# A dense SwiGLU layer whose gate and up products are formed, for 12 of 22 blocks, with seven block products in place of eight

## What is computed

```python
def swiglu(h, w_gate, w_up, w_down):          # h 512 x 1024, gate and up 1024 x 2816, down 2816 x 1024
    return (jax.nn.silu(h @ w_gate) * (h @ w_up)) @ w_down
x = x + swiglu(rmsnorm(x, norm_ffn[0]), ffn_w_gate[0], ffn_w_up[0], ffn_w_down[0])
```

## Time and profile before

| what | value |
|---|---|
| median of 3 runs | 1556.56 us (1556.38 to 1557.34) |
| the profiled execution: its time | 1556.81 us |
| its span (first to last instruction) | 1555.1 us |
| PE busy | 1538.5 us, 99% of the span |
| DVE, ACT, POOL busy | 65%, 54%, 15% |
| granted TensorE clock | 0.997 of full |

### The profile page before, as it was taken

The page is one execution under the profiler, slowest core; times in us unless marked ns, Lnnn a source line. Parts: engine busy times, 40 slices in busy tenths (PEclk is TensorE's granted clock), DMA queues, the critical chain, the costliest instruction groups (busy, mean ns, idle before and its releaser), DMA issues.

```text
span 1555.1 us, 23275 instructions
## 1 busy us (share of the span) xinstructions
PE 1538.5 (99%) x7960; PEld 1309.2 (84%) x7961; DVE 1009.2 (65%) x1689; ACT 834.3 (54%) x1330; POOL 236.7 (15%) x290
## 2 busy tenths in 40 slices
PE   9999999999999999999999999999999999999997
PEld 6888888888888888888888888879898888889895
DVE  7657765755444443336557765776676988887587
ACT  6436665433223322324447664475576888886564
POOL 0204564000000000002015662010000011110000
PEclk9999999999999999999999999999999999999998
DMA  7832212244444233326322212518778999997773
GB/s 228 196 99 69 74 55 82 95 136 136 156 138 138 95 91 98 99 91 155 102 92 69 72 55 90 195 57 320 257 256 254 358 385 372 388 384 266 240 255 134
DMA packets 89787, 265.71 MB, mean 171 GB/s; under 512 B 12497, under 2 KB 22737, under 8 KB 89680
## 3 DMA queue, kind: packets, MB, share of 16 engines
q1 hardware_dynamic: 82864, 248.59, 47.1%
q0 software_dynamic: 6816, 15.74, 3.7%
HBM read 242.84 MB, written 19.83 MB: 169 GB/s over the span
## 4 chain that ended last, share of the span: by engine, by line
PE 96%; DVE 2%; DMA 1%; issue 1%; ACT 0%; SPq 0%; DVEq 0%; ACTq 0%; POOLq 0%
PE ps L1698 19%; PE ps L1703 19%; PE ps L1699 19%; PE ps L2052 8%; PE ps L2027 5%; PE ps L2029 5%; PE ps L2028 5%; PE ps L2054 3%; PE ps L1865 2%; PE ps L1898 1%; PE ps L2026 1%; PE ps L2025 1%; PE ps L1878 1%; PE ps L1897 1%; PE ps L1877 1%; PE ps L2013 1%
## 5 line engine op out<-in xcount | busy, mean ns | idle before, releaser
L808 ACT ACTIVATE w_hi<-raw 128x1024 fp32r<-128x1024 f32 (+1 forms) x168 | 176.0, 1047 | 337.1 <-PE ps L1703 333.8
L1698 PE MATMUL ps<-h_hi,w_hi 128*128 128x512 f32 x880 | 350.6, 398 | 0.6 <-DVE k_lo L1245 0.4
L1699 PE MATMUL ps<-h_lo,w_hi 128*128 128x512 f32 x880 | 343.6, 390 | 0.0
L1703 PE MATMUL ps<-h_hi,w_lo 128*128 128x512 f32 x880 | 343.4, 390 | 0.0
L1157 DVE TENSOR_TENSOR w_lo<-raw,w_hi 128x1024 fp32r<-128x1024 f32 x136 | 164.3, 1208 | 124.1 <-ACT w_hi L808 123.9
L1162 DVE TENSOR_TENSOR m_lo<-m_raw,m_hi 128x1024 fp32r<-128x1024 f32 x144 | 167.9, 1192 | 61.1 <-ACT m_hi L851 60.3
L1703 PEld LDWEIGHTS ps<-h_hi,w_lo 128*128 128x128 f32 x880 | 165.2, 188 | 35.4
L1698 PEld LDWEIGHTS ps<-h_hi,w_hi 128*128 128x128 f32 x880 | 165.6, 188 | 27.0 <-DVE k_lo L1245 0.8
L1699 PEld LDWEIGHTS ps<-h_lo,w_hi 128*128 128x128 f32 x880 | 166.0, 189 | 25.9 <-issue 0.7
L851 ACT ACTIVATE m_hi<-m_raw 128x1024 fp32r<-128x1024 f32 x144 | 145.4, 1031 | 53.0 <-PE ps L2026 25.9
L2052 PE MATMUL ps<-xt,m_hi 128*128 128x320 f32 x592 | 154.3, 347 | 0.3 <-issue 0.3
(11 more groups left out here) (308 smaller groups left out, 3161.7 us busy)
## 6 DMA issues: line engine op xcount, KB each, us to landing
m_raw<-moe_g SPq DMA_DIRECT2D x88, 512.0 KB, 5.1
raw<-w_in SPq DMA_DIRECT2D x68, 512.0 KB, 3.4
m_raw<-moe_down SPq DMA_DIRECT2D x56, 512.0 KB, 5.2
raw<-w_gu SPq DMA_DIRECT2D x44, 512.0 KB, 3.5
h_rows<-moe_g SPq DMA_DIRECT2D x32, 512.0 KB, 5.2
h_rows<-moe_g SPq DMA_DIRECT2D x32, 384.0 KB, 4.6
h_rows<-moe_down SPq DMA_DIRECT2D x24, 512.0 KB, 5.7
m_raw<-moe_g SPq DMA_DIRECT2D x24, 384.0 KB, 5.6
```

The lines of the kernel that those rows point to most:

```text
L808: A.activation(split_of(n, 0, cols)[0], raw[:, n % RAW, 0:cols], ACT.Copy).then_inc(hi_ready, 1)
L1698: E.matmul(ps[:, bank, :], wh, hi, start=first, stop=False)
L1699: E.matmul(ps[:, bank, :], wh, lo, start=False, stop=False)
L1703: return E.matmul(ps[:, bank, :], wl, hi, start=False, stop=final)
```

## The change

Twelve of the 22 pairs (f = 3, 4, 6, 7, 9, 10, 12, 13, 15, 16, 18, 19: two in turn, then one as before) are computed as a product of two-by-two blocks. The weights are split into gate and up, and each into its lower and upper half of the width; the tokens' h into lower and upper width, and into the first and second 256 tokens. With sums of weights (three tiles of 128x512: u_lo + u_hi, that minus g_lo, g_lo - u_lo, and later g_hi minus the second) and sums of tokens (four tiles of h, made once) seven products of half the width and half the tokens give the four results by additions. A block product is 4 width blocks by 3 matmuls of 128x256.

- PE: a pair of this kind ("seven") is 7 products of 12 matmuls of 128x256; a pair of the old kind stays 48 matmuls of 128x512.
- POOL makes the three sums of weights and the later fourth, and the low part of the sixth product's weights (number 5 of 0 to 6): per pair 5 instructions of 128x512.
- ACT makes seven high parts of 128x512 in place of two of 128x1024, and copies the first product's result out of PSUM (128x256).
- DVE makes the other six low parts of 128x512, and four additions (one of 128x256, three of 128x512) that read PSUM. The gate is scaled by rms_inv in place (from SBUF), the up result is not scaled; the factor is multiplied into the result of the down product instead (8 further 128x512 in PSUM, one per three down units). The work on silu and act of the two pairs stands behind the second one.
- The w_hi and w_lo buffers are handed out by halves: a block product's weights are split when the product three before it begins. The two raw buffers of a seven come free together, after its last low parts.
- The whole h (eight 128x512, ACT) and its four sums (two of 128x1024 on DVE, two on POOL) are made during pairs 0 to 2, and split into high and low (eight of 128x512 on ACT and on DVE).

The core of the diff:

```diff
+        SEVENS = [f for f in range(PLAIN, KF - 2) if (f - PLAIN) % 3 < 2]
+        JOBS = [job for f in range(KF) for job in
+                ([("seven", f, j) for j in range(7)] if f in SEVENS else [("unit", f, j) for j in range(2)])]
...
+        def seven_weights(f, j):
+
+            gate, up = FFN_START + 2 * f, FFN_START + 2 * f + 1
+            low, high = slice(0, T), slice(T, UNIT)
+            return ((gate, low), (None, 1), (None, 2), (None, 0), (gate, high), (up, high), (None, 2))[j]
...
             def load(n, src):
-                if n >= RAW:
-                    sp.wait_ge(lo_ready, n - RAW + 1)
+                m = n - RAW
+                if FFN_START + 2 <= m < FFN_END:
+                    f, j = (m - FFN_START) // 2, m % 2
+                    if f in SEVENS:
+                        sp.wait_ge(seven_lo, low_by(f))
+                        sp.wait_ge(seven_lo_pool, SEVENS.index(f) + 1)
+                    else:
+                        sp.wait_ge(seven_lo, LOW_COUNT[JOB[("unit", f, j)]])
+                elif n >= RAW:
+                    sp.wait_ge(lo_ready, m + 1)
                 sp.dma_start(raw[:, n % RAW, 0:src.shape[1]], src).then_inc(raw_full[n % RAW], 16)
...
+            def weight_sums(q, part):
+
+                f = SEVENS[q]
+                n = FFN_START + 2 * f
+                gate, up = raw[:, n % RAW, :], raw[:, (n + 1) % RAW, :]
+                split = lambda p, j: LOW_COUNT[JOB[("seven", SEVENS[p], j)]]
+                if part == 0:
+                    pool.wait_ge(raw_full[n % RAW], 16 * (n // RAW + 1))
+                    pool.wait_ge(raw_full[(n + 1) % RAW], 16 * ((n + 1) // RAW + 1))
+                    if q:
+                        pool.wait_ge(seven_lo, split(q - 1, 3))
+                    pool.tensor_tensor(sums[0][:], up[:, 0:T], up[:, T:UNIT], ALU.add).then_inc(sums_ready, 1)
+                    pool.wait_ge(sums_ready, 4 * q + 1)
+                    pool.tensor_tensor(sums[1][:], sums[0][:], gate[:, 0:T], ALU.subtract).then_inc(sums_ready, 1)
+                if part == 1:
+                    if q:
+                        pool.wait_ge(seven_lo, split(q - 1, 6))
+                    pool.tensor_tensor(sums[2][:], gate[:, 0:T], up[:, 0:T], ALU.subtract).then_inc(sums_ready, 1)
+                if part == 2:
+                    pool.wait_ge(sums_ready, 4 * q + 2)
+                    pool.wait_ge(seven_lo, split(q, 2))
+                    pool.tensor_tensor(sums[2][:], gate[:, T:UNIT], sums[1][:], ALU.subtract).then_inc(sums_ready, 1)
+
+            def low_on_pool(q):
+
+                x = JOB[("seven", SEVENS[q], 5)]
+                pool.wait_ge(seven_hi, x - 1)
+                hi, lo = job_split(x)
+                pool.tensor_tensor(lo, job_full(x), hi.bitcast(F32), ALU.subtract).then_inc(seven_lo_pool, 1)
...
+                if layer == 0:
+                    pool.wait_ge(h32_ready, KD)
+                    pool.wait_ge(t_full_ready, 2)
+                    pool.tensor_tensor(t_full(2), h_block(0, second_half), h_block(0, first_half), ALU.subtract).then_inc(t_full_ready, 1)
+                    pool.tensor_tensor(t_full(3), h_block(1, first_half), t_full(0), ALU.subtract).then_inc(t_full_ready, 1)
+                    for part in range(3):
+                        weight_sums(0, part)
+                    for q in range(1, len(SEVENS)):
+                        if q % 2:
+                            weight_sums(q, 0)
+                            low_on_pool(q - 1)
+                        else:
+                            low_on_pool(q - 1)
+                            weight_sums(q, 0)
+                        weight_sums(q, 1)
+                        weight_sums(q, 2)
+                    low_on_pool(len(SEVENS) - 1)
...
+                    def whole_h(k):
+                        A.activation(h_full(k), xs[:, k, :], ACT.Copy, scale=gains[:, gain_of(1), k:k + 1]).then_inc(h32_ready, 1)
+
+                    for k in range(KD - 2):
+                        whole_h(k)
+                    for x, (kind, f, j) in enumerate(JOBS):
+                        if x < 2:
+                            A.wait_ge(unit_done, FFN_START + x + 1)
+                        else:
+                            A.wait_ge(seven_done, x - 1)
+                        if kind == "seven" and j == 0:
+                            A.activation(quarters[:, 4 * f, :], seven_bank(f, 0), ACT.Copy).then_inc(p1_kept, 1)
+                        for y in FREED_BY[x]:
+                            job_high(y)
+                        if x >= len(JOBS) - 2:
+                            first_down(FFN_END + x - len(JOBS) + 2)
+                        if kind == "seven" and j == 6 and f + 1 not in SEVENS:
+                            silu(f - 1)
+                            silu(f)
+                            act_hi(f - 1)
+                            act_hi(f)
+                        if kind == "unit" and j == 0:
+                            silu(f)
+                        if x == 0:
+                            whole_h(KD - 2)
+                            whole_h(KD - 1)
+                        if kind == "unit" and j == 1 and f + 1 not in SEVENS:
+                            act_hi(f)
+                        if kind == "seven" and j == 0 and f - 1 not in SEVENS:
+                            act_hi(f - 1)
+                        if x in (3, 4):
+                            token_parts_hi((2 * x - 6, 2 * x - 5))
...
+                        if kind == "seven" and j == 1:
+                            V.wait_ge(p1_kept, q + 1)
+                            if q % 2:
+                                V.wait_ge(seven_sums, 4 * q)
+                            V.tensor_tensor(quarters[:, 4 * f + 2, :], quarters[:, 4 * f, :], banks[:, 2, :], ALU.add).then_inc(seven_sums, 1)
+                        if kind == "seven" and j == 3:
+                            V.wait_ge(seven_sums, 4 * q + 1)
+                            V.tensor_tensor(quarters[:, 4 * f + 1:u3_at(f) + 1:u3_at(f) - 4 * f - 1, :], twice(quarters[:, 4 * f + 2, :]),
+                                            banks[:, 4:7:2, :], ALU.add).then_inc(seven_sums, 1)
+                        if kind == "seven" and j == 5:
+                            V.wait_ge(seven_sums, 4 * q + 2)
+                            u3 = quarters[:, u3_at(f), :]
+                            if f + 1 < KF - 2:
+                                V.tensor_tensor(quarters[:, 4 * f + 2:4 * f + 4, :], twice(u3), banks[:, 3:5, :], ALU.add).then_inc(seven_sums, 1)
...
+                        if kind == "seven" and j == 6:
+                            V.tensor_tensor(quarters[:, 4 * f:4 * f + 2, :], quarters[:, 4 * f:4 * f + 2, :], banks[:, 1:8:6, :], ALU.add).then_inc(seven_sums, 1)
+                        for y in FREED_BY[x]:
+                            if not on_pool(y):
+                                job_low(y)
+                        if x >= len(JOBS) - 2:
+                            split_lo(FFN_END + x - len(JOBS) + 2)
+                        if kind == "seven" and j == 6 and f + 1 not in SEVENS:
+                            V.wait_ge(seven_sums, 4 * (q + 1))
+                            gate_scaled_in_place(f - 1)
+                            gate_scaled_in_place(f)
+                            gated_up(f - 1, act_of(f - 1))
+                            gated_up(f, act_of(f))
+                            act_lo(f - 1)
+                            act_lo(f)
+                        if kind == "unit" and j == 1:
+                            gated_up(f, ps[:, pair_banks(f)[1], :])
+                            if f + 1 not in SEVENS:
+                                act_lo(f)
+                        if kind == "seven" and j == 1 and f - 1 not in SEVENS:
+                            act_lo(f - 1)
+                        if x == 1:
+                            V.wait_ge(h32_ready, KD)
+                            V.tensor_tensor(t_full(1), h_block(1, second_half), h_block(0, second_half), ALU.subtract).then_inc(t_full_ready, 1)
+                            V.wait_ge(t_full_ready, 1)
+                            V.tensor_tensor(t_full(0), t_full(1), h_block(0, first_half), ALU.add).then_inc(t_full_ready, 1)
+                        if x in (3, 4):
+                            token_parts_lo((2 * x - 6, 2 * x - 5))
...
+                            scaled(ps[:, m % 2, :], m % 2).then_inc(ffn_scaled, 1)
+                            V.wait_ge(ffn_scaled, KF + m + 1)
                             V.tensor_tensor(xs[:, m, :], xs[:, m, :], ps[:, m % 2, :], ALU.add).then_inc(x_updated, 1)
...
+                    def block_product(x, f, j):
+                        q, out = SEVENS.index(f), seven_bank(f, j)
+                        if j == 0 and q % 2 == 0:
+                            E.wait_ge(ffn_scaled, f)
+                        if j == 1 and q == 0:
+                            E.wait_ge(act_ready, 1)
+                        if j == 3 and q % 2 == 0:
```

(24 more changed lines are left out.)

199 lines of the change are left out of this document (156 added, 43 removed).

## The result

| | time, median (lowest to highest), us | runs | ratio to before, 95% |
|---|---|---|---|
| before, beside it | 1556.55 (1556.38 to 1557.34) | 6 | |
| changed | 1562.46 (1560.02 to 1564.78) | 6 | 1.0037 [1.0024, 1.005] |

What follows compares the result with a forecast made beforehand. PE, busy on 99% of the span, was taken to bound the kernel. Against the profiled 1556.81 us, -11.7 + 0.8 + 4.5 + 5.5 + 0.7 = -0.2 gave 1556.6; median forecast 1556.4, range 1546 to 1562.

Steps and rivals of the forecast that it cites:

- PE's own time: Gate and up stage: twelve sevens of 84 short matmuls at 0.118 us each save 11.7 us.
- entry (a), third unit: Pairs 0 to 3: six ACT copies of h delay the third unit's high part; PE waits 0.8 us.
- entry (b), pair 1: DVE and POOL need 11.8 us in pair 1 where PE takes 10.9: 0.8 us late.
- entry (b), first block products: Four token low parts on DVE lie before the splits of the first block products: 1.3 us late.
- entry (b), first L806: POOL's first low part for product 5 stands behind sums that began late: about 2.4 us.
- five waits before product 5: First seven of two, five of six groups: POOL's low part comes late, 1.1 us each, 5.5 us (0 to 8.5).
- the down scaling at the end: Scaling the down result lengthens the chain to the next layer's first unit by 0.7 us (0.6 to 0.9).
- The hold: DVE instructions with two SBUF inputs and POOL instructions reading SBUF block each other; each POOL one takes about 1.6 us.
- Rival 1: No blocking between DVE's and POOL's two-input instructions: -10.2 us, 1546.4 us; chance 0.22.
- rival 3: DVE and POOL go strictly in turn, PSUM work included: 9.6 us of waits for 5.5, 1560.5 us; chance 0.09.
- rival 4: DVE and POOL block each other, but less: rhythm waits 0.5 us, entry 2, total 1550.9 us; chance 0.20.
- Rival 2: Long runs of short matmuls settle at 0.1245 us each: saving 5.2 us for 11.7, 1562.9 us; chance 0.12.

Runs made afterwards that it cites:

- experiment 3: Changed kernel with POOL's five instructions per seven replaced by equally long zero writes that read nothing; only the stage compares: 353.17 us, 10.2 below the changed kernel.
- experiments 2 and 7: 2: changed kernel with POOL's low part always before the next seven's first sums, 1554.42 us; 7: that plus POOL's token sums as zero writes, stage 353.11 us.
- experiment 4: Changed kernel without the eight scalings of the down result: 1560.32 us, ratio 1.0024 to the kernel before.

## Why the prediction was wrong

Term by term, in us of the stage; measured from start distances in the first profile. The median missed the forecast by 6.1 us; the stage of the first profile missed the sum by 3.1 of them.

| term of the sum | forecast | measured |
|---|---|---|
| PE's own time, 1008 matmuls | -11.7 | -10.3 |
| entry (a), third unit | 0.8 | 1.0 |
| entry (b), pair 1 | 0.8 | 1.3 |
| entry (b), first block products | 1.3 | 1.3 |
| entry (b), first L806 | 2.4 | 2.6 |
| five waits before product 5 | 5.5 | 6.3 |
| the down scaling at the end | 0.7 | 0.5 |
| not found | 0 | 0.2 |
| sum | -0.2 | +2.9 |

- **The mechanism in the stage was right.** The hold exists for instructions with two SBUF inputs (experiment 3), PSUM work passes beside it, and the waits stand where the forecast put them, those before product 5 ended by the instruction that it named. Rival 1 (no hold) and rival 3 (strictly in turn) are out; so is rival 4, since the waits were larger than the forecast's and not smaller. That rival 2's time, 1562.9, is next to the measured median is chance: its condition, 0.1213 us a matmul, was not met.
- **The step that failed is "PE's own time", the saving of 11.7 us; 10.3 were measured.** It is the largest single error of the sum. I took 0.118 from four matmuls in a row, though the three behind the first stood at 0.120 in the same group. Long runs give 0.1194. The difference of 0.0014 was multiplied by 1008: 1.4 of the 3.1 us. Rival 2's mechanism (a long run settles higher) was partly true, at a fifth of its size: 0.1245 was foretold by it, 0.1194 came.
- **Waits were priced without their restart.** Behind each wait the next distance is 0.22 for 0.12 (or 0.34 for 0.23). That is 0.10 each, about 1 us over the ten waits, of the 1.7 us by which entry and rhythm are above their forecast. The wait in the rhythm itself was nearly right: 1.17 measured, 1.1 foretold.
- **Pair 1 was 1.3 instead of 0.8.** The forecast added up the whole work of DVE and POOL over the pair. What PE waited for was one low part, and experiments 2 and 7 show what made it late: beside POOL's sums of 2.40 and 3.38 us two low parts took 6.46, and with writes in their place 1.21 and 2.27.
- **The end was right for the edit** (0.70 by experiment 4) and 0.2 high for the sum, since the wait of 0.15 that was there before would have gone anyway: without the scaling PE does not wait there.
- **A term was missing: the clock.** The forecast kept PE at the full clock of the earlier trace rows. In two of the four profiles of the changed kernel the granted clock is at 0.5 (1.2 GHz) for 3.4 us behind the wait of 2.3 us, and the stage is 1.5 us longer.
- **What stays open.** The four profiled executions took 1560.2 to 1561.2 us. That is accounted for: 2.9 in the stage, 1.5 where the clock fell, and a rest of the program that varies by 1 to 2. The medians, 1562.5 and 1562.4, lie 1 to 2 us above them all, and two executions took 1564.6 and 1564.8 at a mean clock of 0.995 and 0.996. More than one fall of the clock would fit these two, but one of 1562.7 had 0.998, and no profile caught an execution over 1561.2. So 1 to 2 of the 6.1 us stay open.
- **As to the range:** its upper end of 1562 held the profiled executions, but not what comes on top of them in the median. It was said to end short of rivals 2 and 3, though rival 3's 1560.5 is inside it; and it had no allowance for each of ten places costing a little more.
